# First layer: VectorE scales a head pair's softmax and masks its stick weights each in front of a weight block's low part, and takes the stick output last

## What is computed

```python
# softmax heads, per block of 128 queries
p_a = softmax(where(chunk_ok, q_a @ k_a.T * scale_a, -inf));  out_a = p_a @ v_a
# stick-breaking heads
z = q_b @ k_b.T * scale_b
log_keep = where(before, log_sigmoid(-z), 0)
log_between = cumsum(log_keep, reverse=True) - log_keep
w_b = where(before, exp(log_sigmoid(z) + log_between), 0)
out_b = w_b @ v_b
h = h + concatenate([out_a, out_b]) @ w_out
```

## Time and profile before

| | |
|---|---|
| median of three runs | 1368.72 us (1364.67 to 1371.44) |
| the profiled execution, own time | 1366.44 us |
| its span (first to last instruction) | 1364.7 us |
| busy: PE, DVE, ACT, POOL | 1293.0, 815.4, 732.7, 371.6 us |
| granted TensorE clock, mean over the span | 0.982 of full |
| the stage of the change | about 48 to 141 us of the span |

### The profile page before, as it was taken

One profiled execution on the slowest core, in us unless ns is written; L12 is line 12 of the kernel. 1 busy time (PEld: TensorE's weight loads), 2 busy tenths in 40 slices (PEclk: granted clock), 3 DMA queues, 4 the chain that ended last, 5 costly groups with the idle time before them and its releaser, 6 DMA issues.

```text
span 1364.7 us, 28476 instructions
## 1 busy us (share of the span) xinstructions
PE 1293.0 (95%) x10337; PEld 1232.9 (90%) x10337; DVE 815.4 (60%) x1434; ACT 732.7 (54%) x1337; POOL 371.6 (27%) x414
## 2 busy tenths in 40 slices
PE   5988999999999999999978799999998998999999
PEld 5967899999998899999967489999998877999999
DVE  5666655566576655567689646555546565755544
ACT  6554666655455666656445545444435565644433
POOL 1011244421000244421312106771000220487300
PEclk9999999999999999999999689999999899999999
DMA  7522465566654455566523015556555432555665
GB/s 252 163 93 94 140 193 185 186 205 201 197 184 147 140 185 184 184 205 201 164 65 123 31 46 172 174 178 186 170 171 166 132 125 82 153 187 184 199 187 156
DMA packets 62725, 217.97 MB, mean 160 GB/s; under 512 B 7968, under 2 KB 10032, under 8 KB 62512
## 3 DMA queue, kind: packets, MB, share of 16 engines
q1 hardware_dynamic: 60304, 210.20, 48.9%
q10 hardware_dynamic: 2336, 6.58, 1.5%
HBM read 215.68 MB, written 1.08 MB: 159 GB/s over the span
## 4 chain that ended last, share of the span: by engine, by line
PE 66%; DVE 13%; issue 11%; ACT 6%; POOL 4%; DMA 1%; POOLq 0%; SPq 0%; ACTq 0%; DVEq 0%
PE bank L330 19%; PE bank L332 19%; PE bank L331 19%; DVE wlo L314 3%; DVE ulo L398 2%; ACT whi L309 2%; ACT prob L1000 1%; POOL scratch L569 1%; POOL scratch L567 1%; DVE prob L991 1%; PE bank L964 1%; PE bank L949 1%; POOL alo L571 1%; PE bank L946 1%; DVE h L501 1%
## 5 line engine op out<-in xcount | busy, mean ns | idle before, releaser
L314 DVE TENSOR_TENSOR wlo<-raw,whi 128x1024 fp32r<-128x1024 f32 (+1 forms) x394 | 480.2, 1219 | 169.3 <-ACT whi L309 169.0
L330 PE MATMUL bank<-uhi,whi 128*128 128x256 f32 (+1 forms) x1848 | 535.1, 290 | 19.0 <-DVE wlo L314 13.9
L332 PE MATMUL bank<-uhi,wlo 128*128 128x256 f32 (+1 forms) x1848 | 526.5, 285 | 0.0
L331 PE MATMUL bank<-ulo,whi 128*128 128x256 f32 (+1 forms) x1848 | 525.8, 285 | 0.0
L309 ACT ACTIVATE whi<-raw 128x1024 fp32r<-128x1024 f32 (+1 forms) x394 | 410.6, 1045 | 189.8 <-PE bank L332 184.3
L330 PEld LDWEIGHTS bank<-uhi,whi 128*128 128x128 f32 x1848 | 351.4, 190 | 27.6 <-issue 20.7
L332 PEld LDWEIGHTS bank<-uhi,wlo 128*128 128x128 f32 x1848 | 351.7, 190 | 0.0
L331 PEld LDWEIGHTS bank<-ulo,whi 128*128 128x128 f32 x1848 | 350.2, 189 | 0.7
L330 PE MATMUL bank<-ahi,whi 128*128 128x256 f32 (+1 forms) x1176 | 336.6, 286 | 2.6 <-DVE wlo L314 1.6
L332 PE MATMUL bank<-ahi,wlo 128*128 128x256 f32 (+1 forms) x1176 | 334.1, 284 | 0.0
L331 PE MATMUL bank<-alo,whi 128*128 128x256 f32 (+1 forms) x1176 | 333.6, 284 | 0.0
(11 more groups left out here) (228 smaller groups left out, 1253.3 us busy)
## 6 DMA issues: line engine op xcount, KB each, us to landing
raw<-stream SPq DMA_DIRECT2D x394, 512.0 KB, 3.6
scratch<-decay ACTq DMA_DIRECT2D x8, 416.0 KB, 3.5
scratch<-relh ACTq DMA_DIRECT2D x8, 384.0 KB, 3.4
constants<-consts SPq DMA_DIRECT2D x1, 1360.0 KB, 11.9
h<-xT SPq DMA_DIRECT2D x4, 256.0 KB, 4.0
out<-h SPq DMA_DIRECT2D x8, 128.0 KB, 3.6
h<-metaT SPq DMA_DIRECT2D x1, 64.0 KB, 11.5
gain_columns<-gains SPq DMA_DIRECT2D x1, 45.0 KB, 1.9
```

What stands on the lines that cost most here:

```text
L314: dve.tensor_tensor(wlo[:, s, 0:w], raw[:, s, 0:w], whi[:, s, 0:w].bitcast(F32), ALU.subtract).then_inc(w_lo, 1)
L330: pe.matmul(dst, hi, a, start=first and i == 0, stop=False)
L331: pe.matmul(dst, hi, b, start=False, stop=False)
L332: mm = pe.matmul(dst, lo, a, start=False, stop=last and i == chunks - 1)
```

## The change

In DVE's list alone, in every round: the scalings of the pair before (`pair_scale_dve`) move from behind the first m unit to in front of it; `stick_weights_dve` moves from behind unit k to in front of it; `stick_out_dve` moves from in front of the row maxima to behind them.

```diff
@@ mix_dve
             for s in range(4):
-                unit("m", 2 * s)
                 if s > 0:
                     pair_scale_dve(dve, link, mla, s - 1)
+                unit("m", 2 * s)
                 stick_split_dve(dve, s, 0)
                 unit("m", 2 * s + 1)
                 stick_split_dve(dve, s, 1)
...
                 if s > 0:
                     out_lo(dve, mla, s - 1)
                 stick_arg_dve(dve, s)
+                stick_weights_dve(dve, s)
                 if s < 3:
                     unit("k", s + 1)
-                stick_weights_dve(dve, s)
-                stick_out_dve(dve, s)
                 for i in (2 * s, 2 * s + 1):
                     biased_max_dve(dve, mla, i)
+                stick_out_dve(dve, s)
             pair_scale_dve(dve, link, mla, 3)
             out_lo(dve, mla, 3)
```

## The result

The changed kernel took 1349.16 us as the median of four runs (1346.53 to 1352.18), the kernel before 1367.74 us in four (1364.67 to 1371.44). The ratio is 0.9869 with a 95% interval of 0.9848 to 0.9889: faster by 1.3%, or 18.6 us between the medians. The forecast was faster, 1355.5 us with a range of 1350.0 to 1361.6. Over all sixteen runs of the changed kernel the mean is 1352.2 us, and over sixty-five of the kernel before it is 1367.1: 14.9 us, or 1.1%.

The account below looks back on a forecast made before the run. TensorE was taken as the bound, busy 1293.0 of 1364.7 us. Three rounds 10.4, clock 1.5 and tail 1.1 us sum to 13.0; from the median 1368.7 that gives 1355.7, stated as 1355.5, range 1350.3 to 1361.6.

Parts of the forecast that it names:

- Step 1: Masked stick weights ahead of unit k: masks fill DVE's idle time, TensorE's waits at the stick values go, 2.3 us.
- Step 2: Stick output behind the row maxima: ACT's exponentials start 1.9 us earlier, the output stays hidden with 1 us of cover.
- Step 3: Scalings ahead of DVE's low part and evacuation: fit with 0.2 us to spare, 2.5 us idle at the transposes vanish.
- Step 5: Tail, round 3: exponentials and scalings of pair 3 come earlier, so the second head's transposes do too, 1.1 us less.
- Step 4: TensorE's granted clock no longer falls in unit q of round 1: 1.5 us less, bounds 0 and 4.6 us.
- A: Half the gain: exponentials start no earlier, TensorE waits in front of unit q; 7.1 us less, 1361.6 us; chance 0.08.
- B: No change that can be told: TensorE's wait moves whole to unit q, only 2.3 us won, 1366.4 us; chance 0.05.
- C: Slower: the clock falls in the denser rounds and stays down, 1384 us; chance 0.02.

## Why the prediction was right or wrong

- **Step 1, the masked weights.** Right: the waits at L1547 are gone, and the masks cost nothing. Alone they are worth 2.7 us of stage (0.3 more than I gave them, in a profile with one fall as before).
- **Step 2, the stick output.** Right: the exponentials start 0.28 us after the start of ACT's copy, 1.96 us sooner than in the kernel before (70.36 less the 0.55 of the later begin is 69.81, against 71.77). The move alone shortens the stage by 6.2 us, in which the clock's 1.6 are contained.
- **Step 3, the scalings.** Right, cover of 0.2 us included. No wait in front of unit q shows. The second and third stretch from stick argument to stick argument, which had no fall, became 3.7 and 3.5 us shorter where I had 3.47. In round 1 unit q starts 3.71 us sooner (75.24 - 0.55 against 78.40): 0.80 us were won at the stick values and not 0.76, 0.30 at the two heads' transposes and not 0.24, and 0.1 more between these two. The wait of round 3 stayed, at 0.96 us.
- **Step 5, the tail.** Right: from the stick arguments of round 3 to the second head's transposes 7.22 us, where it was 8.36.
- **Step 4, the clock.** The mechanism was right, the size too small. I took the one fall of the one profile that I had. Three profiles of the kernel before show one, three and one, for 1.6, 3.3 and 1.6 us against the stage with the waits filled (140.6). By these the term is some 2.2 us (an estimate, the mean of three), with 3.3 us and not 4.6 as its upper end. The changed stage has no falls in three profiles.
- **The range, the step that failed.** The stage's gain was forecast as 13.0 us and measured as 13.66 in the first pair of profiles, and as 14.2 with the means of three. The time missed the range because of "I see nothing that takes it back": I put the 1200 us behind the stage at no change at all. They vary by 4 us with the same program, by falls of the clock in the sparse attention and elsewhere. The 6.3 us from 1355.5 to 1349.16 are made up so: 0.7 of stage, 2.8 behind it in the profiled pair, less 0.7 for the later start and the time outside the span; 2.1 us that I had added because the first execution before lay under its median; and 1.5 by which the profiled execution after lay above its own. So the stage accounts for a tenth of the 6.3 us; the rest is the part behind it and the choice of executions. And I built the low end, 1350.3, from one execution of 1366.4 us (the high end from the median of 1368.7), while the runs shown ahead of the prediction went down to 1364.7; with that alone it would have been 1348.6. That the time fell outside was in part chance: the first four runs of the changed kernel were the lower part of what it does, the next twelve had medians of 1353.3 and 1354.1, and both these and the mean of all sixteen lie inside the range.
- **The rivals.** A, the exponentials that start no sooner, was built as the run with only the scalings moved: 0.88 us of wait in front of unit q of round 1, where the forecast's times give 0.85 (transposes done at 75.7, unit q from 76.55). It didn't occur in the full change. B and C didn't occur.

## What to carry to other kernels

Where engines run hand-written lists and one splits weights ahead for another, the split of a unit that is needed three steps later should not stand in front of the two short instructions that the bound engine waits for; put each short step where the engine would idle for its partner anyway, and check in the trace that it ends before that partner does. Marks in the profile on both sides of a stage show a change of 0.5 us that the whole time hides in a scatter of 10 us. An idle stretch of the matrix engine is to be priced twice, for itself and for the clock behind it, with a range from no fall to all.

## What the runs showed of the hardware

- TensorE's clock fell to its 1.2 GHz level behind, or at the very end of, idle stretches of 2.4 to 2.5 us: in one of three cases in two profiles and in three of three in another, with the same program, and in one of three in the run with only the masked weights moved. In two of these six falls the granted clock was down before TensorE had begun its first transpose. Behind stretches of 1.2 to 1.3 us it did not fall (six cases in two profiles). With TensorE busy on matmuls whose result nobody reads, it did not fall in six cases.
- The kernel before has times from 1359.6 to 1372.3 us, and they go with the mean granted clock: runs at 0.986 took 1359.6 to 1361.7 us, runs at 0.978 took 1367.4 to 1370.1, and runs at 0.975 took 1370.3 to 1372.3. Behind the stage all fourteen profiled executions run the same code, and it took from 1198.8 to 1206.7 us. A comparison of four runs with four can be off by some us here.
- The plain float32 matmuls of the extra work (128 x 128 by 128 x 256) show as two records each: ten of them, 20 records, took 4.48 us, and five, 10 records, took 2.32 us, at a clock of 1.00.
